# Two layers in one program, norm gains as rows, and all modulation chunks between feed-forward chunks

## What is computed

```python
for l in range(DEPTH):                              # 2 layers
    h = rms_norm(x, norm_mix_pre[l])
    proj = h @ w_in[l]
    ...                                             # attention, conformer and pooling branches
    gates = jax.nn.sigmoid((h @ w_gate[l]).reshape(bsz, seq, N_BRANCH, D_MODEL))
    mix = jnp.einsum("bsnd,bsnd->bsd", gates, up) @ w_o[l]
    x = x + rms_norm(mix, norm_mix_post[l])
    hf = rms_norm(x, norm_ffn_pre[l])
    u = causal_depthwise_conv(hf @ ffn_w_up[l], ffn_conv_w[l], ffn_conv_b[l])
    gate, val = jnp.split(u, 2, axis=-1)
    f = (jax.nn.gelu(gate, approximate=True) * val) @ ffn_w_down[l]
    x = x + rms_norm(f, norm_ffn_post[l])
```

```python
sh_a, sc_a, g_a, sh_f, sc_f, g_f = [m[:, None, :] for m in jnp.split(silu_c @ w_mod[l] + b_mod[l], 6, axis=-1)]
mod_c = jnp.split(silu_cc @ w_mod[l][:, :n_mod * D_MODEL] + b_mod[l][:n_mod * D_MODEL], n_mod, axis=-1)
```

## Time and profile before

| | us |
|---|---|
| three runs | 1990.0, 1981.78, 1986.79 |
| median | 1986.79 |
| the profiled execution | 1983.36 |
| its span | 1981.6 |
| mean granted clock of TensorE | 0.927 |

### The profile page before, as it was taken

How to read it: one execution, slowest core, us unless ns; L and a number is a source line. 1 busy time by engine, 2 the same in 40 slices (tenths; PEclk the granted TensorE clock), 3 DMA queues, 4 the chain that set the end, 5 groups by cost and what they waited for, 6 DMA issues and landing times. The chain is left out here.

```text
span 1981.6 us, 26811 instructions
## 1 busy us (share of the span) xinstructions
PE 1793.0 (90%) x10780; PEld 1450.1 (73%) x10780; DVE 1076.1 (54%) x1478; ACT 754.2 (38%) x1055; POOL 351.9 (18%) x313
## 2 busy tenths in 40 slices
PE   6898998899996898999899998999899896899996
PEld 5786788599965687779599974545476646799995
DVE  4567776466533667866466621165554407355545
ACT  4344554455423344464355530123114402333441
POOL 0222213034400212312025400012320001000000
PEclk9998999799996999999889997899969997799998
DMA  5452324645554452334645555222100032245541
GB/s 222 160 192 87 127 107 151 242 159 184 189 219 155 162 192 104 110 107 170 233 147 186 191 191 220 106 71 78 43 22 1 1 136 77 106 179 183 191 175 79
DMA packets 39390, 279.99 MB, mean 141 GB/s; under 512 B 4464, under 2 KB 4720, under 8 KB 6384
## 3 DMA queue, kind: packets, MB, share of 16 engines
q1 hardware_dynamic: 37984, 272.44, 38.1%
q10 hardware_dynamic: 1296, 6.00, 0.8%
HBM read 277.37 MB, written 1.05 MB: 141 GB/s over the span
## 5 line engine op out<-in xcount | busy, mean ns | idle before, releaser
L395 DVE TENSOR_TENSOR ring_low<-ring,sb_hi 128x2048 fp32r<-128x2048 f32 (+1 forms) x118 | 243.8, 2066 | 271.0 <-ACT sb_hi L388 271.0
L388 ACT ACTIVATE sb_hi<-ring 128x2048 fp32r<-128x2048 f32 x118 | 225.6, 1912 | 287.7 <-DMA ring<-weights 143.6
L532 PE MATMUL psum<-sb_hS,sb_hi 128*128 128x256 f32 x704 | 202.9, 288 | 5.5 <-DVE ring_low L395 4.2
L781 PE MATMUL psum<-sb_hfT,ring_low 128*128 128x256 f32 x704 | 198.9, 282 | 0.0
L535 PE MATMUL psum<-sb_hS,sb_hi 128*128 128x256 f32 x704 | 198.5, 282 | 0.0
L536 PE MATMUL psum<-sb_hS,ring_low 128*128 128x256 f32 x704 | 197.5, 281 | 0.0
L1743 DVE TENSOR_TENSOR sb_split<-ring,sb_split 128x2048 fp32r<-128x2048 f32 x48 | 110.0, 2292 | 160.1 <-ACT sb_split L1738 160.1
L2036 PE MATMUL psum<-sb_hfS,sb_split 128*128 128x256 f32 x512 | 146.4, 286 | 2.4 <-PE psum L2058 2.0
L532 PEld LDWEIGHTS psum<-sb_hS,sb_hi 128*128 128x128 f32 x704 | 133.3, 189 | 17.8 <-issue 11.3
L2040 PE MATMUL psum<-sb_hfS,sb_split 128*128 128x256 f32 x512 | 145.9, 285 | 0.0
L2039 PE MATMUL psum<-sb_hfS,sb_split 128*128 128x256 f32 x512 | 145.9, 285 | 0.0
(11 more groups left out here) (382 smaller groups left out, 4222.5 us busy)
## 6 DMA issues: line engine op xcount, KB each, us to landing
ring<-weights SPq DMA_DIRECT2D x256, 1024.0 KB, 4.8
sb_rows<-rows ACTq DMA_DIRECT2D x1, 2048.0 KB, 9.0
sb_cols<-cols ACTq DMA_DIRECT2D x2, 694.0 KB, 6.3
sb_rows<-rows ACTq DMA_DIRECT2D x2, 516.0 KB, 6.8
sb_x<-x_in SPq DMA_DIRECT2D x1, 1024.0 KB, 4.8
sb_rows<-rows ACTq DMA_DIRECT2D x2, 512.0 KB, 9.4
sb_y<-ctx_in SPq DMA_DIRECT2D x1, 1024.0 KB, 10.7
out<-sb_x SPq DMA_DIRECT2D x2, 512.0 KB, 2.6
```

The source lines that it names most:

```text
L388: act.activation(hi_of(n), ring[:, c % SLOTS, :], ACT.Copy).then_inc(hi_ready, 1)
L395: eng.tensor_tensor(low_of(n)[:, half], ring[:, SPLIT_CHUNKS[n] % SLOTS, half], hi_of(n)[:, half].bitcast(F32), ALU.subtract)\
L532: mm = pe.matmul(out, hi[:, k, bs], hS[:, 0, k, :], start=(k == 0), stop=False)
L781: mm = pe.matmul(out, lo[:, k, b * P:(b + 1) * P], hfT[:, 0, k, :], start=False, stop=(k == KD - 1))
```

## The change

- The two layers are written out one behind the other in one program; no barrier and no loop jump stand between them. The loads of the next layer's gains and columns and the high and low parts of its first two chunks are issued inside the layer before (`next_heads`).
- Norm gains are rows broadcast to all partitions. DVE multiplies x with the gain row while the root is being made; ACT scales token tile 0, DVE tile 1; POOL makes the root of each tile apart; transposes go tile by tile. The square of the norm behind a product reads PSUM, DVE multiplies PSUM with the gain row, and one instruction scales and adds to x.
- At the start of the kernel ACT splits chunks 0 and 1 before it squares x, and DVE makes their low parts before it multiplies with the gain.
- Down chunks hold four blocks of 128 x 512 of one output half; inside a chunk the token tile is the outer loop.
- The pad chunk moves from gate 8 to gate 12, the conformer's transposes (`obT`) go earlier, the mix's high and low parts go among the last branch chunks, and ACT's copies c0, c1 and qT go ahead of the high part of chunk `FIRST_BA + 1`.
- All 12 modulation chunks of a layer stand in the feed-forward loop: the halves of step i behind chunks 3i+1 and 3i+2, its turn behind chunk 3i+4. ACT's copy (now `mod_out`, L878 of the new kernel) is in step 3i+3, DVE's addition (`mod_in`, L1129) in step 3i+6.

The diff, cut to its core (line numbers of the new kernel are others: L413 is its `split_hi`, L420 its `split_lo`, L488 `mod_half`, L501 `mod_turn`, L814 to L818 feed-forward, L836 to L840 down, L1075 and L1080 ACT's two operations of a feed-forward step):

```diff
-MODS_WO, MODS_DOWN = range(0, MOD_STEPS // 2), range(MOD_STEPS // 2, MOD_STEPS)
-PAD_GATE = 8
+MOD_AFTER_FFN = {3 * i + h + 1: (i, h) for i in range(MOD_STEPS) for h in range(2)}
+TURN_AFTER_FFN = {3 * i + 4: i for i in range(MOD_STEPS)}
+PAD_GATE = 12
...
-    for i, r in zip(MODS_WO, "tus"):
...
+    for i, r in zip(range(MOD_STEPS), 2 * ("s0", "s1", "t")):
+        jobs.plan(("mod", i), r)
+        jobs.plan(("modT", i), r)
...
+            jobs.plan(("down", c, t), ("s0", "s1", "t", "u")[2 * t + c])
...
-            for i in MODS_WO:
-                mod_half(i, 0)
-                mod_half(i, 1)
-            for i in MODS_WO[:-1]:
-                mod_turn(i)
...
-            mod_turn(MODS_WO[-1])
-            pe.wait_ge(h_lo, 4 * TT)
+        turn_normed("hf", 2)
...
+            if j in MOD_AFTER_FFN:
+                mod_half(*MOD_AFTER_FFN[j])
+            if j in TURN_AFTER_FFN:
+                mod_turn(TURN_AFTER_FFN[j])
...
+            hi, lo = (part.rearrange("p (q n) -> p q n", q=BLOCKS) for part in next_split())
+                ts = slice(t * P, (t + 1) * P)
+                for q in range(BLOCKS):
+                    c, n = divmod(BLOCKS * i + q, FB)
+                    name = ("down", c, t)
+                    if n == 0:
+                        jobs.claim(pe, name)
...
+        def norm_first(turn):
+            act.wait_ge(xg_ready, 2 * turn + 1)
+            act.wait_ge(rstd_ready, 4 * turn + 1)
+            act.activation(tm[:, 0, :], tm[:, 0, :], ACT.Copy, scale=rstd[:, 0:1]).then_inc(normed_act, 1)
...
+        split_hi(act, FIRST_BA)
             for i in range(2):
-                split_hi(act, FIRST_BA + i)
                 copy_out(("c", i), cpad[:, 2 * i:2 * i + 2, 16:16 + T], jobs.out(("c", i)).rearrange("p (b t) -> p b t", b=2))
             for t in range(TT):
                 copy_out(("qT", t), qTs[:, 0, :, t * P:(t + 1) * P], jobs.out(("qT", t)).rearrange("p (m t) -> p m t", m=4), 0.125)
+        split_hi(act, FIRST_BA + 1)
...
+            act.activation(scratch_of[t], jobs.out(name), ACT.Square, accum_out=ss4[:, t, c:c + 1]).then_inc(post_sq, 1)
...
                 if j < FB:
+                if MOD_AFTER_FFN.get(j - 1, (0, 0))[1] == 1:
+                    mod_out(MOD_AFTER_FFN[j - 1][0])
                     split_hi(act, FIRST_FFN + j + HI_FFN)
...
+            jobs.drain(dve.tensor_tensor(tm[:, t, cs], jobs.out(name), R["post_mix" if kind == "wo" else "post_ffn"][:, cs], ALU.mult), name)
...
+                dve.scalar_tensor_tensor(out=x[:, t, :], in0=tm[:, t, :], scalar=rstd[:, 2 + t:3 + t], in1=x[:, t, :],
+                                         op0=ALU.mult, op1=ALU.add).then_inc(x_ready, 1)
...
                 split_lo(dve, FIRST_FFN + j + HI_FFN)
+            if j - 2 in TURN_AFTER_FFN:
+                mod_in(TURN_AFTER_FFN[j - 2])
...
-            with nc.Fori(0, LAYERS) as l:
-                layer_block(nc, l, mem1, ring, ring_low, landed, used, weights, psum, sems, cols, rows, loaded, placed)
+                @block.scalar
+                def _(act):
+                    layers[0]["heads"]["load_pre"](act)
+                    layers[0]["heads"]["load_cols"](act)
+                    layers[0]["heads"]["highs"](act)
+                    for layer, next_heads in zip(layers, heads):
+                        layer["scalar"](act, next_heads)
```

More of the change, by code:

```diff
@@ L250, in plan_layer @@
         for i in range(4):
[L251 to L253 removed]
+            if (n, i) in OB_BEFORE:
+                jobs.plan(("obT", OB_BEFORE[(n, i)]), drains=4)
             jobs.plan(("up", n, i))
@@ new lines, in load_pre, with load_cols, highs_head, lows_head @@
+    def load_pre(act):
+        load_rows(act, "pre_mix", D, R["pre_mix"], pre_in)
+    def load_cols(act):
+        act.dma_start(cols[:, :], cols_dram[l]).then_inc(cols_in, 16)
+        load_rows(act, "sinks", 8, R["sinks"], sinks_in)
+    def highs_head(act):
+        split_hi(act, 0)
+        split_hi(act, 1)
+    def lows_head(dve):
+        split_lo(dve, 0)
+        split_lo(dve, 1)
+    def sync_program(sp):
+        with sp.Fori(0, N_LAYER_CHUNKS // SLOTS) as turn:
+            for s in range(SLOTS):
+                sp.wait_ge(used[s], l * (N_LAYER_CHUNKS // SLOTS) + turn + 1)
+                sp.dma_start(ring[:, s, :], wts[l * N_LAYER_CHUNKS + turn * SLOTS + (s + SLOTS)]).then_inc(landed[s], 16)
@@ L550, in hid_half @@
-            def hid_half(kv, half):
-                chunk = next_chunk().rearrange("p (l h) -> p l h", l=8)
-                if half == 0:
-                    jobs.claim(pe, ("hid", kv))
-                    pe.wait_ge(flat_ready, 4 * kv + 5)
-                for lp in range(8):
-                    mm = pe.matmul(jobs.out(("hid", kv))[32 * (lp % 4):32 * (lp % 4) + 32, 0:T], flat32[:, kv, 8 * half + lp, :],
-                                   chunk[:, lp, :], start=(half == 0 and lp < 4), stop=(half == 1 and lp >= 4))
-                    if lp == 0:
-                        carry(mm)
-                if half == 1:
-                    jobs.fill(mm, ("hid", kv))
-                release(("hid", kv))
@@ new lines, in scalar_program @@
+        split_hi(act, FIRST_GATE)
+        copy_out("gaT", small[:, 0:48], jobs.out("gaT")[:, 0:48], func=ACT.Sigmoid)
+        copy_out(("bg", 1), sg[:, 1, :], func=ACT.Sigmoid)
+        for t in range(TT):
+            copy_out(("rqT", t), qTs[:, 1, :, t * P:(t + 1) * P], jobs.out(("rqT", t)).rearrange("p (m t) -> p m t", m=4), 0.125)
+            copy_out(("rdT", t), qTs[:, 2, :, t * P:(t + 1) * P], jobs.out(("rdT", t)).rearrange("p (m t) -> p m t", m=4), 0.125)
+        split_hi(act, FIRST_GATE + 1)
@@ new lines, in out_copy, with turned_out @@
+        def out_copy(i):
+            a, t, g = ITEMS[i]
+            if a > 0 and g == 1:
+                copy_out(("O", a, t), brS[(0, 0, 3)[a]][:, 0, :, t * P:(t + 1) * P], jobs.out(("O", a, t)).rearrange("p (m t) -> p m t", m=4))
+        def turned_out(i):
+            a, t, g = ITEMS[i]
+            for kb in range(t + 1):
+                copy_out(("PT", a, t, g, kb), pt[:, i % 2, kb, :, :], jobs.out(("PT", a, t, g, kb)).rearrange("p (j q) -> p j q", j=4))
+        exps(0)
+        gate_out(1)
@@ new lines, in pool_low @@
+        def pool_low():
+            for i in range(2):
+                region, _, before, _ = jobs.jobs[("pool", i)]
+                dve.wait_ge(drained[region], before + 2)
+                for b in range(2):
+                    n = 2 * i + b
+                    jobs.drain(dve.scalar_tensor_tensor(out=brS[2][:, 1, n, :], in0=jobs.out(("pool", i))[:, b * T:(b + 1) * T],
+                                                        scalar=C("pool_s", n, n + 1), in1=brS[2][:, 0, n, :].bitcast(F32),
+                                                        op0=ALU.mult, op1=ALU.subtract), ("pool", i))
@@ new lines, in out_low @@
+        def out_low(i):
+            a, t, g = ITEMS[i]
+            if a > 0 and g == 1:
+                region, _, before, _ = jobs.jobs[("O", a, t)]
+                part = brS[(0, 0, 3)[a]][:, :, :, t * P:(t + 1) * P]
+                dve.wait_ge(drained[region], before + 1)
+                jobs.drain(dve.tensor_tensor(part[:, 1, :, :], jobs.out(("O", a, t)).rearrange("p (m t) -> p m t", m=4),
+                                             part[:, 0, :, :].bitcast(F32), ALU.subtract), ("O", a, t))
@@ L2807, in build_program @@
+            nums = [s.num for s in layer_sems]
+            assert nums == list(range(nums[0], nums[-1] + 1))
+            nc.all_engine_barrier(sems_to_clear=range(nums[0], nums[-1] + 1))
         with ExitStack() as second:
```

1961 lines of the change are left out of this document (995 added, 966 removed).

## The result

The changed kernel takes 2083.6 us in the median of four runs (2080.2 to 2086.2), the kernel before 1986.4 beside it. The ratio is 1.049, with a 95% interval of 1.047 to 1.051: **4.9% slower**. The forecast was 2056 with a range of 2018 to 2085, slower. The profiled execution of the changed kernel has a span of 2082.5, 100.9 longer than before.

The account below looks back on a forecast made before the run. PE bounds the kernel, busy for 90% of the span, so time is its work plus its gaps. 1983.4 (profiled) - 94 of gains + 5 at the start + 162 added over two layers = 2056 us, range 2018 to 2085.

Parts of the forecast that it names:

- The wait: Feed-forward loop: PE stands 7.8 us for ACT's modulation copy at turns 0 to 4, 39.0 a layer.
- 4.94 with the release: In the feed-forward wait: from the first matmul carrying a slot's release to the high part awaiting the transfer, 4.94 us.
- The clock: Behind each feed-forward wait: 2.1 us lost, 10.5 a layer; bounds 1.5 (turn counts as work) and 2.7 (it doesn't).
- The modulation chunks themselves: Between feed-forward chunks: twelve modulation chunks add 0.93 us each to PE, 11.1 a layer.
- The chunk f3: Feed-forward chunk behind two modulation chunks: PE waits 1.6 to 1.9 us a layer for its landing and splits.
- The first down chunk: Second token tile waits 6.6 us for the PSUM region of modulation step 5; 8.7 with a cold clock.
- rkT: Before the first wo chunk: copying first removes PE's transpose wait of 6.4 and a cold clock, 15 us in two layers.
- The first wo chunk: Two of four low parts move ahead; of a 3.3 wait 0.8 stays, gaining 8 us with the cold clock.
- Start: Kernel start: ACT splits two chunks before squaring x, so the first projection begins at 24.5 to 26 for 19.98, +5.
- The gains: Shorter norm chains at boundaries: wo to feed-forward 15.4 us a layer, between layers 28, into the second block 12.
- Rival C: Norm chain gains come short: each of five boundaries keeps 6 more, +30, 2086 us; chance 0.11.
- Rival A: Feed-forward: modulation hides, the turn's copy is there when PE wants it; 1955 us, faster by 1.4%; chance 0.07.

Follow-up runs that it names:

- the copy first: Changed kernel with ACT's copy of a modulation row ahead of the high part that waits for a transfer, all else the same: 1993.1 us, 1.003 to before.
- the later turn: Changed kernel with PE's turn of step i behind chunk f(3i+5) instead of f(3i+4), DVE's addition one step later: 2002.0 us, 1.008 to before.
- the run with the three small edits: Changed kernel with ACT squaring x before its splits, DVE copying rkT before the low part, modulation steps 1, 2, 4, 5 in other regions: 2040.4 us.
- the last experiment: Changed kernel with copy first, start, rkT and region edits, modulation behind feed-forward chunks 1, 3 ... 21 and down chunk 1, turns later: 1924.3 us, 0.969 to before.

## Why the prediction was right, and where it was off

**The wait.** The largest term was named with its place, its links, its count and nearly its size: 39.0 of standing a layer, measured 44.2 (8.9, 8.7, 8.7, 9.0, 8.9) and 0.6 more at the sixth turn. The mis-sized link is "4.94 with the release": I took it from a chunk whose release rides on a first matmul of 0.28. In the changed kernel the release of f(3i+4) rides on the first of the modulation chunk's matmuls, and the transfer is issued 1.2 behind its start, when the chunk's eight rows are through (L488 x8, 1.07). The two rows of SP that this rests on, from the kernel before, behind a feed-forward chunk's first matmul at 408.98 and a modulation chunk's at 583.11:

```profile
409.08 0.33 SPq L406 DMA_DIRECT2D ring<-weights  x1
```

```profile
584.33 2.04 SPq L406 DMA_DIRECT2D ring<-weights  x3
```

Two runs attacked the wait from opposite ends of the loop, without a change in transfers: the copy first took all of it away, the later turn 6.8 of each 8.8 in layer 1, as expected. This cause is shown.

**The clock.** 2.1 for each wait, measured 1.3 to 2.7 (the chunk behind took 7.2 to 8.6 for 5.9), 1.8 in the mean. Against that, chunk f0 no longer starts cold: it and f1 take 11.5, where they took 13.9. Windows of the changed kernel over the wait, the turn, and the chunk behind in three pieces:

```profile
416.74:425.61 8.87, 0.00 (x0) 0.03 (x1) 1.81 (x1) 3.61 (x5) 0.55 (x1) 0.75 0.32 118
425.61:427.45 1.84, 1.84 (x9) 1.84 (x9) 1.84 (x5) 0.00 (x0) 1.70 (x3) 0.50 0.22 31
427.31:429.30 1.99, 1.99 (x10) 1.99 (x11) 0.34 (x1) 0.00 (x0) 0.65 (x1) 0.50 0.84 292
429.30:431.30 2.00, 2.00 (x12) 2.00 (x11) 0.00 (x0) 0.00 (x0) 0.00 (x0) 0.50 0.57 229
431.30:435.06 3.76, 3.76 (x35) 3.63 (x38) 0.67 (x1) 2.62 (x3) 0.00 (x0) 0.98 0.01 2
```

The granted clock falls inside the wait (0.75 in the mean), is 0.50 through the turn and the first 4 us of f5, and then full. The turn itself takes 1.84 there for 1.02 warm (at 575.16), so that 2.6 are lost from the end of the wait on, 0.8 in the turn and 1.8 behind it. That is about what f0 lost before, with no turn between its gap and it (2.7), and what the down loop loses behind its wait of 6.8, 2.7 to 3.0 (71.0 less 6.8, for 61.2 in the run with the three small edits). So the rows fit a turn that counts as work, the forecast's bound of 1.5; no run tried it apart. The worked example of the Trainium skill's page "TensorE: Matmul & The Clock Gate" (section "HAM oscillation — how this bites in real kernels") has 1.67 us throttled a turn of its loop, by which I had estimated 0.83 lost. The rows say 1.8, and the measurement decides.

**The modulation chunks themselves** cost more than the 0.93 that I took from three in a row. From a chunk's first matmul to that of the feed-forward chunk behind it it is 1.0 (392.23 to 393.23), and the feed-forward chunk ahead of it takes 5.86 (393.23 to 399.09) for 5.62: 1.2 each, some 7 us over both layers.

**The chunk f3** waited 2.5, not 1.9 (the same 1.2 of a late release), and then took 1.5 more at the low clock, which I had left out. **The first down chunk** waited 6.8, forecast 6.6, and the stretch grew by 9.5 and 9.2, forecast 8.7.

**rkT: the step that failed.** "The change copies first and splits later. Gain 6.4 and a cold clock" was read from ACT alone. The copy of rkT is DVE's, behind a low part that wants the same chunk, and it came as late as before (10.2 us behind the transposes, 10.5 before), so next to nothing was gained: a wait of 7.5 for one of 6.4, and the work that PE had behind the old wait now ahead of the new one. Of the 15 us that the forecast took off for it, 0.3 a layer came. I had the order of both engines and looked at one.

**The first wo chunk** waits 1.3 for 3.3, forecast 0.8. And a wait of the kernel before that the forecast did not name is gone, in a branch chunk:

```profile
PE psum L729 <- DVE ring_low L395: 2.4, 1, 2.4
```

So the stretch up to the first wo chunk is 5.8 and 6.0 shorter, for the 11.6 of the forecast, though rkT gave almost nothing.

**Start:** +7.1 for +5. Chunk 1 landed at 16.5 (high part at 16.56), above my bound of 15.22; a gain row of 512 KB now lands ahead of it, and that this delays it is my reading. POOL's two root operations took 1.2 and 1.4 where I had 0.9 for both.

**The gains** at the boundaries came nearly as forecast: 14.7 and 14.4 for 15.4, 26.7 for 27.8, 11.8 for 12. Rival C had next to no share. Rival A, the modulation that hides, is what the last experiment built: it asked for another order, and then the modulation hides but for PE's own work on it, 1924.

**The sum:** by the table, 2056 + 2 (start) + 11 (first projection to wo) + 14 (feed-forward) + 2 (wo to feed-forward) + 1.5 (down loop) + 1.5 (boundary and way into the second block) - 1 (wo chunks) - 3 (second block, which I had at nothing) = 2084. The 14 of feed-forward are, over both layers, 11 for the waits (the release that comes 1.0 later ten times), 7 for the modulation chunks' own work and 4 for f3, less 3 for the clock and 5 for f0. So three terms carry the miss: the release, rkT, and the length of a modulation chunk; that they partly cancel against terms I left out or put too high is luck, and 2083.6 is only just inside the range that ends at 2085. The second block's -3.1 was not looked into.
